# Reordering the delta-rule block ahead of its triangular inversion in a two-layer encoder trunk on one Trainium2 core

## The reference

```
x = x + 1/2 * SwiGLU_1(RMSNorm(x))                     # 1024 -> 2816 -> 1024
h = RMSNorm(x)
[q|k|v|g_out|a|b|glu|gates] = h @ w_in
y_A = W_a_out( gated DeltaNet(short conv of q, k, v; decay per head) )
y_B = W_b_out( GLU -> causal depthwise conv(31) -> RMSNorm -> swish )
x = x + W_o( sigmoid(gate_A) * y_A + sigmoid(gate_B) * y_B )
x = x + 1/2 * SwiGLU_2(RMSNorm(x))
```

## Time and profile before

| what | value |
|---|---|
| median of 3 runs | 3130.84 us (3127.74 to 3131.71) |
| the profiled execution, its own time | 3128.97 us |
| its span in the trace | 3127.0 us |
| PE busy | 2904.1 us (93%) |
| DVE busy | 1812.1 us (58%) |
| ACT busy | 1000.1 us (32%) |
| POOL busy | 537.9 us (17%) |
| DMA | 238.04 MB, mean 76 GB/s |
| mean granted PE clock | 0.973 of full |

### The profile page before, as it was taken

How to read it: one execution, slowest core, us unless ns; L and a number is a source line. 1 busy time by engine, 2 the same in 40 slices (tenths; PEclk the granted TensorE clock), 3 DMA queues, 4 the chain that set the end, 5 groups by cost and what they waited for, 6 DMA issues and landing times.

```text
span 3127.0 us, 41087 instructions
## 1 busy us (share of the span) xinstructions
PE 2904.1 (93%) x14080; PEld 2401.0 (77%) x14080; DVE 1812.1 (58%) x2475; ACT 1000.1 (32%) x1519; POOL 537.9 (17%) x308
## 2 busy tenths in 40 slices
PE   7999968988898999999999998788898889999999
PEld 6888847777777888888778886577777778888887
DVE  5554248989787445553255531589888873455532
ACT  3332233433343233232132321333334342333321
POOL 1000034333334010000000000433333330100000
PEclk9999989999999999999999999899999999999999
DMA  4333221211322343333233334333223325333332
GB/s 143 97 94 93 70 75 43 53 48 47 45 49 48 95 100 88 96 99 92 79 101 94 95 95 60 61 54 49 47 49 45 47 54 101 95 90 98 92 93 70
DMA packets 463079, 238.04 MB, mean 76 GB/s; under 512 B 10389, under 2 KB 461077, under 8 KB 462965
## 3 DMA queue, kind: packets, MB, share of 16 engines
q1 hardware_dynamic: 462964, 236.70, 31.3%
HBM read 234.57 MB, written 2.10 MB: 76 GB/s over the span
## 4 chain that ended last, share of the span: by engine, by line
PE 66%; issue 16%; DVE 8%; POOL 5%; DMA 3%; ACT 1%; DVEq 0%; POOLq 0%; SPq 0%; ACTq 0%
PE bank L409 65%; POOL w_lo L1478 3%; DMA raw<-in_w_in 2%; DVE cacc L1178 2%; PE bank L537 1%; DVE ka L1204 1%; DVE va L1204 1%; DVE X L1237 1%; ACT w_hi L746 0%; POOL attn L1551 0%; DVE dcol L1106 0%; POOL qd L1540 0%; POOL decs L1533 0%; DVE NT L1284 0%; POOL attn L1534 0%
## 5 line engine op out<-in xcount | busy, mean ns | idle before, releaser
L409 PE MATMUL bank<-h_hi,w_hi 128*128 128x512 f32 x2432 | 968.7, 398 | 29.8 <-DVE sqb L1215 16.5
L409 PE MATMUL bank<-h_lo,w_hi 128*128 128x512 f32 x2432 | 983.6, 404 | 0.0
L409 PE MATMUL bank<-h_hi,w_lo 128*128 128x512 f32 x2432 | 963.9, 396 | 0.0
L994 DVE TENSOR_TENSOR w_lo<-raw,w_hi 128x1024 fp32r<-128x1024 f32 x336 | 412.3, 1228 | 554.1 <-ACT w_hi L746 553.2
L746 ACT ACTIVATE w_hi<-raw 128x1024 fp32r<-128x1024 f32 x448 | 471.9, 1057 | 696.0 <-PE bank L409 636.4
L409 PEld LDWEIGHTS bank<-h_hi,w_hi 128*128 128x128 f32 x2432 | 463.1, 190 | 124.0 <-DVE sqb L1215 17.4
L409 PEld LDWEIGHTS bank<-h_hi,w_lo 128*128 128x128 f32 x2432 | 463.9, 191 | 84.0
L409 PEld LDWEIGHTS bank<-h_lo,w_hi 128*128 128x128 f32 x2432 | 464.0, 191 | 82.7
L1178 DVE SCALAR_TENSOR_TENSOR cacc<-c_raw,ncol,cacc 128x512 f32<-128x512 f32 x464 | 386.7, 833 | 8.2
L1478 POOL TENSOR_TENSOR w_lo<-raw,w_hi 128x1024 fp32r<-128x1024 f32 x112 | 284.2, 2540 | 505.3 <-ACT w_hi L746 505.3
L1486 POOL TENSOR_TENSOR ssq<-ssq,sqb 128x512 f32<-128x512 f32 x42 | 54.1, 1288 | 1478.0 <-ACT sqb L754 1478.0
(11 more groups left out here) (236 smaller groups left out, 3271.8 us busy)
## 6 DMA issues: line engine op xcount, KB each, us to landing
raw<-in_w_in SPq DMA_DIRECT2D x128, 512.0 KB, 8.0
raw<-in_ffn_w_gate SPq DMA_DIRECT2D x88, 512.0 KB, 3.7
raw<-in_ffn_w_up SPq DMA_DIRECT2D x88, 512.0 KB, 3.7
raw<-in_ffn_w_down SPq DMA_DIRECT2D x64, 512.0 KB, 3.6
raw<-in_ffn_w_down SPq DMA_DIRECT2D x32, 384.0 KB, 3.1
raw<-in_w_a_out SPq DMA_DIRECT2D x16, 512.0 KB, 3.7
raw<-in_w_b_out SPq DMA_DIRECT2D x16, 512.0 KB, 3.7
raw<-in_w_o SPq DMA_DIRECT2D x16, 512.0 KB, 3.7
```

What stands on the lines that cost most here:

```text
L409: return nc.tensor.matmul(o, a, b, start=start, stop=stop, **kw)
L994: tt(w_lo[c % SLOTS][:, :], raw[c % SLOTS][:, :], w_hi[c % SLOTS][:, :].bitcast(F32), ALU.subtract).then_inc(lo_v, 1)
```

## The change

The strict mask of the decay (decs on POOL) goes. NT is made by one step from the kk product, the negated factor and dec. The starting inverse is made by ACT writing the identity into XT (XTI) and DVE copying the pairs of NT onto it under a mask, in place of m1 and a subtraction. The broadcast copies for the weights of gr, fb and the norm spreads (gbc, fbc, norm_fbc) go: PE takes one column with step zero as its weights. On DVE, dmin moves ahead of qT, v's activation behind x2T, and oF, ohi and olo of the previous head into the fillers behind levels 0 and 1. PE has 10 halves between gr and xy0 (17 before), 35 in the levels (30 before), and three instead of two ahead of os1, os2 and os3; the two halves ahead of gr were three. The silu gate sg moves behind vn1. On ACT, X2 and level 0 come ahead of the unit-0 steps. On POOL, rk comes first, then the tail's rs, then deci. The diff, cut:

```diff
@@ -84,29 +84,29 @@
-PE_ORDER = "H H H gr H H kt H so kk H H kq vt H H fb H H H H x2t H H H y0 H H H xy0".split()
+PE_ORDER = "H H gr H H kt kk H kq H so H H x2t vt H H y0 fb H H xy0".split()
 for _l in range(1, LEVELS):
-    PE_ORDER += f"H H H xt{_l - 1} y{_l} H H H xy{_l}".split()
+    PE_ORDER += f"H H H H xt{_l - 1} y{_l} H H H xy{_l}".split()
 PE_ORDER += "H H vn0 H H os0".split()
 for _c in range(1, NC):
-    PE_ORDER += f"H H p{_c} H H vn{_c} H H os{_c}".split()
+    PE_ORDER += f"H H p{_c} H H vn{_c} H H H os{_c}".split()
...
-DVE_STEPS = ["hs", "gbc", "kT", "qT", "vT", "dmin", "skE", "rden", "bnk2", "NT", "m1", "x2T", "attnT"]
+DVE_STEPS = ["hs", "kT", "dmin", "qT", "skE", "rden", "bnk2", "neg", "NT", "x2T", "vT", "attnT"]
...
 for _c in range(1, NC):
...
-DVE_TAIL = ["og", "vE", "fbc", "oF", "ohi", "olo"]
-ACT_STEPS = ["thk", "thq", "thv", "sgc", "ksq", "decT", "eg", "kd", "X2", "vs", "Y0"]
+DVE_TAIL = ["og", "vE", "oF", "ohi", "olo"]
+ACT_STEPS = ["thk", "thq", "XTI", "thv", "ksq", "decT", "eg", "kd", "sgc", "X2", "Y0", "vs"]
 for _l in range(1, LEVELS):
...
-POOL_STEPS = ["decs", "deci", "rk", "qd"]
+POOL_STEPS = ["rk", "deci", "qd"]
@@ -310,9 +308,9 @@
...
-        def spread(cols):
-            return cols.rearrange("p (c o) -> p c o", o=1).broadcast_to([P, NC, P])
+        def whole(col):
+            return col.broadcast_to([P, P])
@@ -424,9 +422,9 @@
...
-    pe.wait_ge(fbc_done, nf + 1)
+    pe.wait_ge(rs_done, nf + 1)
@@ -546,9 +544,9 @@
...
-            ve("gbc")
+            ve("hs")
...
-                m = mm(bank[0][:, c * P:c * P + P], dec[:, c * P:c * P + P], incl)
+                m = mm(bank[0][:, c * P:c * P + P], whole(hs[:, HS_G, c:c + 1]), incl)
@@ -611,9 +609,9 @@
...
-            pe.wait_ge(ve_tl.sem, ve_tl.after(rn, "fbc"))
+            pe.wait_ge(po_tl.sem, po_tl.after(rn, "rs"))
...
-                m = mm(bank[5][:, c * P:c * P + P], fbc[:, c, :], ident)
+                m = mm(bank[5][:, c * P:c * P + P], whole(sm[:, 5, c:c + 1]), ident)
@@ -679,9 +677,9 @@
...
+                pe.wait_ge(rs_done, l * 4 + 3)
@@ -860,13 +858,19 @@
...
+        def level(lv):
+            if lv:
+                pe_(f"xt{lv - 1}")
+                nc.scalar.activation(XT[:, :], bank[3][:, :], ACT.Copy).then_inc(*ac_dn.step(f"XT{lv - 1}"))
+            pe_(f"y{lv}")
+            nc.scalar.activation(Y[:, :], bank[1][:, :], ACT.Copy).then_inc(*ac_dn.step(f"Y{lv}"))
         if rn is not None:
             pe_("vn3", rn - 1)
+            nc.scalar.activation(chunked(XT), each_chunk(I_ID), ACT.Copy).then_inc(*ac_dn.step("XTI"))
             act.wait_ge(ve_ds.sem, ve_ds.after(rn, "v3"))
-            nc.scalar.activation(XT[:, :], va[:, :], ACT.Tanh).then_inc(*ac_dn.step("thv"))
-            act.wait_ge(ve_tl.sem, ve_tl.after(rn - 1, "og"))
-            act.wait_ge(ve_ds.sem, ve_ds.after(rn, "sg"))
-            nc.scalar.activation(sgc[:, :], sgn[:, :], ACT.Copy).then_inc(*ac_dn.step("sgc"))
+            nc.scalar.activation(thv[:, :], va[:, :], ACT.Tanh).then_inc(*ac_dn.step("thv"))
             act.wait_ge(po_tl.sem, po_tl.after(rn - 1, "sum"))
             pe_("kt")
             for c in range(NC):
@@ -878,11 +882,16 @@
             for c in range(NC):
                 a = nc.scalar.activation(kd[:, c * P:c * P + P], bank[1][:, c * P:c * P + P], ACT.Copy, scale=hs[:, HS_KD, c:c + 1])
             a.then_inc(*ac_dn.step("kd"))
+            act.wait_ge(ve_tl.sem, ve_tl.after(rn - 1, "og"))
+            act.wait_ge(ve_ds.sem, ve_ds.after(rn, "sg"))
+            nc.scalar.activation(sgc[:, :], sgn[:, :], ACT.Copy).then_inc(*ac_dn.step("sgc"))
+            pe_("x2t")
+            nc.scalar.activation(X[:, :], bank[0][:, :], ACT.Copy).then_inc(*ac_dn.step("X2"))
+            level(0)
         dense_steps(0, *dense)
         if rn is not None:
-            pe_("x2t")
-            nc.scalar.activation(X[:, :], bank[0][:, :], ACT.Copy).then_inc(*ac_dn.step("X2"))
             act.wait_ge(po_dn.sem, po_dn.after(rn, "rk"))
+            pe_("vt")
             for c in range(NC):
                 a = nc.scalar.activation(vs[:, c * P:c * P + P], bank[4][:, c * P:c * P + P], ACT.Copy, scale=sm[:, 3, c:c + 1])
             a.then_inc(*ac_dn.step("vs"))
@@ -890,17 +899,9 @@
...
-        def level(lv):
-            if lv:
-                pe_(f"xt{lv - 1}")
-                nc.scalar.activation(XT[:, :], bank[3][:, :], ACT.Copy).then_inc(*ac_dn.step(f"XT{lv - 1}"))
-            pe_(f"y{lv}")
-            nc.scalar.activation(Y[:, :], bank[1][:, :], ACT.Copy, scale=-1.0).then_inc(*ac_dn.step(f"Y{lv}"))
         for t in range(1, 5):
             if rn is not None:
-                for lv in ((0, 1), (2, 3), (4, 5), ())[t - 1]:
+                for lv in ((1, 2), (3, 4), (5,), ())[t - 1]:
                     level(lv)
@@ -998,13 +999,8 @@
...
-            def norm_fbc(nf):
-    dve.wait_ge(rs_done, nf + 1)
-    nc.vector.tensor_copy(fbc[:, :, :], spread(nrm[:, 1, :])).then_inc(fbc_done, 1)
...
-    norm_fbc(nf)
@@ -1215,15 +1210,17 @@
             stt(out=sgn[:, :], in0=gth[:, :], scalar=1.0, in1=bank[7][:, :], op0=ALU.add, op1=ALU.mult).then_inc(*ve_ds.step("sg"))
-        first = ("t", "t", "t", (0, 0), "t", (0, 1))
-        behind = [("t", (0, 2), "t", "t", "t", "t"), ((1, 0), "t", (1, 1), "t", (1, 2), "t"),
-                  ("t", "t", "t", "t", (2, 0), "t"), ((2, 1), "t", (2, 2), "t", "t", "t"),
-                  ("t", "t", "t", "t", "g", "t"), ()]
+        first = ("t", "t")
+        behind = [("t", (0, 0), "oF", (0, 1), "ohi", (0, 2)), ("olo", "t", "t", "t", "t", "t"),
+                  ("t", (1, 0), "t", (1, 1), "t", (1, 2)), ("t", "t", "t", "t", "t"),
+                  ((2, 0), "t", (2, 1), "t", (2, 2), "t"), ()]
         def put(items):
             for x in items:
-                if x == "t":
+                if x == "t" or x in DVE_TAIL and not (dn and before):
                     fill()
+                elif x in DVE_TAIL:
+                    tail(x, rn - 1, hn - 1)
                 elif x == "g":
                     silu_gate()
                 else:
@@ -1243,65 +1240,56 @@
...
             ts(hs[:, :, :], hsc[:, hn, :, :], 1.0, None, ALU.mult).then_inc(*ve_dn.step("hs"))
-            me("hs")
-            nc.vector.tensor_copy(chunked(dec), spread(hs[:, HS_G, :])).then_inc(*ve_dn.step("gbc"))
             def act_of(n, src, dst, th):
                 ac(f"th{n}")
                 stt(out=dst[:, :], in0=th[:, :], scalar=1.0, in1=src[:, :], op0=ALU.add, op1=ALU.mult).then_inc(*ve_dn.step(f"{n}T"))
             act_of("k", ka, kT, Y)
-            if before:
-                tail("og", rn - 1)
-            act_of("q", qa, qT, X)
-            act_of("v", va, va, XT)
             pe_("gr")
             for c in range(NC):
                 a = ts(dec[:, c * P:c * P + P], bank[0][:, c * P:c * P + P], hs[:, HS_GC, c:c + 1], 0.0, ALU.subtract, ALU.min)
             a.then_inc(*ve_dn.step("dmin"))
+            act_of("q", qa, qT, X)
             if before:
-                tail("vE", rn - 1)
+                tail("og", rn - 1)
             ac("ksq")
...
+            me("bnk2")
+            ts(sm[:, 6, :], sm[:, 2, :], -1.0, None, ALU.mult).then_inc(*ve_dn.step("neg"))
+            me("neg")
+            ac("decT")
+            pe_("kk")
+            for c in range(NC):
...
+                a = stt(out=NT[:, t], in0=bank[2][:, t], scalar=sm[:, 6, c:c + 1], in1=dec[:, t], op0=ALU.mult, op1=ALU.mult)
+            a.then_inc(*ve_dn.step("NT"))
+            me("NT")
+            ac("XTI")
+            dve.sem_inc(xy_seen, 1)
+            nc.vector.copy_predicated(chunked(XT), where(I_M1T), chunked(NT)).then_inc(*ve_dn.step("x2T"))
+            if before:
+                tail("vE", rn - 1)
+            act_of("v", va, va, thv)
             dve.wait_ge(ac_ds.sem, ac_ds.after(rn, "gt_th"))
             dve.wait_ge(taps, rn * TAPS + TAPS)
             stt(out=c_raw[:, TAPS - 1:], in0=gth[:, :], scalar=1.0, in1=valb[:, :], op0=ALU.add, op1=ALU.mult).then_inc(*ve_ds.step("craw"))
-            if before:
-                tail("fbc", rn - 1)
         if dense and dn:
             columns(*dense)
         if dn:
-            me("bnk2")
-            po_("decs")
-            pe_("kk")
-            for c in range(NC):
...
-                a = stt(out=NT[:, t], in0=bank[2][:, t], scalar=sm[:, 2, c:c + 1], in1=decs[:, t], op0=ALU.mult, op1=ALU.mult)
-            a.then_inc(*ve_dn.step("NT"))
-            if before:
-                tail("oF", rn - 1, hn - 1)
-            me("NT")
-            tt(chunked(XT), chunked(NT), each_chunk(I_M1T), ALU.mult).then_inc(*ve_dn.step("m1"))
-            if before:
-                tail("ohi", rn - 1, hn - 1)
-            else:
-                fill()
-            me("m1")
-            tt(chunked(XT), each_chunk(I_ID), chunked(XT), ALU.subtract).then_inc(*ve_dn.step("x2T"))
-            if before:
-                tail("olo", rn - 1, hn - 1)
             pe_("kq")
             po_("deci")
```

(61 more changed lines are left out.)

## The result

The changed kernel takes 3155.5 us (median of 4 runs, 3151.1 to 3160.0), the kernel before 3130.3 beside it: ratio 1.0084, 95% interval 1.0068 to 1.0100. So it is slower by 25 us (0.8%), outside the interval of no change. The forecast was 3171 within 3108 to 3194, and 3152 to 3186 as its own range; slower had the highest chance. The direction and the range were right, the point 15.5 us too high. Of its terms, some were right and some wrong by more than the whole result.

What follows compares the result with a forecast made beforehand. PE was taken to set the time and DVE to set PE's waits. The terms -54.1 + 76.1 + 0 + 22 + 0 - 2 gave +42 on the profiled 3129, so 3171 us, range 3108 to 3194.

Steps and rivals of the forecast that it cites:

- x2T (-54.1; -51.7): PE's wait for x2T, once per head: the whole 54.1 us goes, with 0 to 1 us per head possibly staying.
- gr (+76.1; +60.4): PE's wait ahead of gr: eight taps behind VN3 delay hs, 5.3 us in most heads, +76.1 us in sum.
- 1, 5, 3, 5, 2 and 0 behind the levels make 18: Count of DVE's taps, 2 in first included; it left seven over, so eight between VN3 and hs.
- the gaps behind the branch: DVE idle after its branch at the four loop edges: 18.4 us in sum, in full on top of the taps.
- The levels (0; -46.7): PE's waits at the levels: 3.4 us per head, 54 in all against 52.1 now, so no change.
- My chain of late copies: DVE's copies in the levels: x0 0.9 us late, level 0 1.0, level 2 0.9, level 5 0.6; 3.4 per head.
- the holds fall away: Rival, 25%: DVE against POOL in levels and scan; without holds up to 89 us less, 3104 us with three quarters.
- The scan (+22; +17.8): Taps behind VN0 and VN2 held by POOL's w_lo, delaying S or R: 1.6 us in 14 heads, +22 us.
- The clock (0; +15.4): PE's clock after waits: old and new waits held equal in cost, 0 us, bounds -10 and +20.
- the clock rival: Rival, 10%: PE's clock at the low level after every gr wait, +20 us, 3191 us.
- the prediction's sentence on the Trainium skill: On PE's clock: by that rule every 5.3 us wait ends at 1.2 GHz, the sum some 20 us higher.
- Longer but fewer: Argument on PE's clock: new gr waits are longer but fewer per head than x2T waits, so 0 us.

Runs made afterwards that it cites:

- old_place: The changed kernel with v's activation, c_raw and the copy of the columns put back ahead of NT on DVE: 3186.1 us, ratio 1.0184.
- carried: The changed kernel with leftover taps moved into the scan, two left behind VN3 and the last three done in the next head: 3067.0 us, ratio 0.9794.
- halves_from_levels: The changed kernel with one half from each of levels 1 to 5 moved ahead of gr: 3134.9 us, ratio 1.0019.
- carried_last: As carried, with a fourth tap carried and, in a layer's last head, the taps behind level 4's copy moved into the scan: 3070.7 us, ratio 0.9802.
- busy_wait: The changed kernel plus 16 unused PE matmuls ahead of the wait for hs in every head carrying a predecessor's tail: 3145.7 us, ratio 1.0062.

## Why the prediction was right, and where it was not

*x2T (-54.1; -51.7).* Right, and old_place confirms the stated reason for 27 us of it: what no longer stands ahead. The other 25 were not divided.

*gr (+76.1; +60.4).* Right mechanism, two sizes off. The step "1, 5, 3, 5, 2 and 0 behind the levels make 18" miscounts the last but one list, which holds three taps. That makes seven taps behind VN3, not eight: 5.3 less 0.755 is 4.55, measured 4.75. And the gaps behind the branch, taken over at 18.4 in sum, are 11.2 (2.7 to 2.9 each) in the changed kernel. Why they shrank stays open, but it is not the changed code alone: in carried and the versions built on it, where only two taps stand between VN3 and the branch, they are about 17 again with one of 6. That they stand in full on top of the taps was right. By the Trainium skill (Runtime: NRT & Kernel Launch, Instruction fetch mechanics) a taken branch outside what is prefetched fetches before it goes on, and the four gaps agree. The two branches that leave the loop (at 939.3 and 2502.5 us) have 0.2 us of idle time behind them.

*The levels (0; -46.7).* This is the step that failed worst, and its mechanism, not only its size. I had DVE's backlog per head at 3.4 us behind seven halves; it is a third of a us. halves_from_levels shows that one half per level, 2.3 us of PE work, is worth 28.8 us over 16 heads, 1.8 each, so most of it takes wait away. My chain of late copies added every held step at its full length and let hardly any of it be absorbed, and the forecast rival "the holds fall away" was half true for that: the copies were on time though the holds were all there.

*XT ahead of vn0 (not named; +27.8).* 15 us of it are the last head of each layer, 7.5 each, which I never looked at by itself. There nine fillers more are taps, POOL has sums as well as transfers, and the six taps behind level 4 were put exactly beside them. The rest is about 1.0 us in each other head: DVE comes late to the last copy, and without the last tap ahead of it (carried_last) 0.3 us is left.

*The scan (+22; +17.8).* Right, with the places named right: S0 and S2, 0.70 and 0.57 us for 1.6 in sum expected.

*The clock (0; +15.4).* Wrong in the direction that the clock rival named, and the prediction's sentence on the Trainium skill gave +20. "Longer but fewer" was the argument; the runs show that all twelve waits for hs of more than 4.7 us end at the low level (gr's records then take 2.07 to 2.08 us), and busy_wait that keeping PE at work through the waits is worth some 20 us. About 8 of the 15.4 can be put down to the clock, as a net of what the gr waits cost and what the x2T waits no longer do.

The sum came out near by luck: 46.7 too much at the levels and 47.3 too little (27.8, 15.4 and v's 4.1) cancel, and what is left of the 16.8 us is mostly gr's 15.7. The sign was less so: the chances rested on the gr term, and that held.

## What to carry to other kernels

Count the cost of a wait on PE as the wait plus what the same matmuls take longer behind it: compare PE's busy time at an equal number of matmuls. One long wait per head is worse than several short ones that sum to as much, and leftover work of a helper engine belongs into the places where it waits anyway, even across the boundary of an iteration. When work is moved in PE's order, follow the transfers that its progress starts, and see which step of the other engine they land on; and read the first and the last iteration of a loop by themselves.
